# All blocks of the first modulation as split products, some rounding remainders and sums of squares on GpSimd, and a fifth key unit in the start stage

## The chip, the cores and the metric

One core of one Trainium2 chip. The time is the device time of one execution in microseconds. The kernel before took 2806.58 us in the median of 3 runs (2803.66 to 2813.95). TensorE is called PE in the profile, VectorE DVE, ScalarE ACT, GpSimd POOL, and SyncE SP. SP issues every DMA of the kernel.

## The reference, cut to what matters

Two transformer blocks on 256 tokens of 2048 features. The change touches only the beginning of the first one: the modulation vectors, the RMS norms of the tokens `x` and of the context `ctx`, and the key product.

```python
silu_c, silu_cc = silu(c), silu(c_ctx)[None]
mod_l = split(silu_c  @ w_mod + b_mod, 6)      # w_mod: 2048 x 12288
mod_c = split(silu_cc @ w_mod + b_mod, 6)
hl = rms_norm(x,   norm1_g) * (1 + mod_l[1]) + mod_l[0]
hc = rms_norm(ctx, norm1_g) * (1 + mod_c[1]) + mod_c[0]
zl  = hl @ w_in + b_in                         # w_in: 2048 x 13312
zkv = hc @ w_in[:, K_OFF:G_OFF] + b_in[K_OFF:G_OFF]
```

Only the first third of `w_mod` (`mod[0]` and `mod[1]`, 4096 columns) is needed before `hl` and `hc` exist. Nothing else of the two blocks can start before those.

## The kernel before

All weights come in blocks of 128x1024 f32 (512 KB), one DMA each, in an order that `unit_plan` writes out. A weight block for a token product is called a unit. It is multiplied as a split product: ACT rounds the block to fp32r (`his`, the first part, line 986), DVE subtracts that from the block (`los`, the second part, line 1570), and PE adds up `hi*xh + hi*xl + lo*xh` (lines 531, 533 and 536). PE takes the units in the order of the plan. There are 5 buffers each for `his` and `los`, so ACT waits before unit u until PE has finished unit u-5.

**The start stage.** The plan's first `NSTART` entries are the start stage. It holds the 64 blocks of the first third of `w_mod`, in 8 rounds of 8 blocks (one round for each `nb` of `MOD0 = (0, 4, 1, 5, 2, 6, 3, 7)`, q = 0 to 7 inside it), and the first halves of the first `NLEAD = 4` key units (`w_in` 40 to 43). The order before is 48 blocks (rounds 0 to 5), key unit 40, round 6, key unit 41, round 7, key units 42 and 43; then come the second halves of the same four units and everything else. I number plan entries b0, b1, and so on.

A round is computed in one of two ways, block by block (lines 612 to 646):

- q = 2 and q = 5 (`WHOLE`, 16 blocks, name `mod0`): PE takes the f32 block as it landed, with a 128x2 stationary operand, two f32 matmuls of 512 columns (line 627). Their end frees the block's buffer (`s_m0p`).
- the other six (48 blocks, name `mods`): split like a unit. PE multiplies `hi` and `lo` with the four columns of `CS` (the two silu vectors, each in two parts), four fp32r matmuls of 512 columns (line 639). The second part's end on DVE frees the buffer (`s_lo`).

After a round, ACT copies four rows out of PSUM (`mrow`, line 1048), PE turns them into columns (`mod0_turn`, line 603, eight small matmuls into the bank `XB`), and DVE adds `b_mod` (`modv`, lines 1668 and 1669).

**The norms.** ACT squares `x` and then `ctx`, four pieces of 128x1024 each (line 1034, `squares`). PE sums them over partitions with a matrix of ones: 16 f32 matmuls of 256 columns for `x` and 16 for `ctx` (line 589, into `XB`). ACT takes the root (line 1016), DVE the reciprocal (line 1650), and DVE multiplies the 16 feature rows (line 1656). Modulation (line 1700 on DVE, 1063 on ACT, 1681 on DVE) then makes four feature rows at a time, in four groups g = 0 to 3; group g needs rounds 2g and 2g+1 of `MOD0` order. The first half of a key unit needs groups 0 and 1, the second half groups 2 and 3.

**What sets the order.** Every engine runs a fixed program. Small tasks are generators that `Ticks.tick` moves on by one step after each plan entry, so a task's place in an engine's queue is the entry number at which its step falls. `early_times` says how many first parts (ACT, `AHEAD = 3` entries ahead) and second parts (DVE, 2 ahead) stand before the tick of an entry. The raw blocks go round 9 buffers in the start stage and 4 after it; SP issues the DMAs in plan order and waits before each for the buffer's last reader. The four `acc` banks, `S0`, `S1`, `TB` and `XB` are the eight PSUM banks. GpSimd has nothing to do in the start stage; its first work is the addition of attention masks much later (line 2338).

Of the kernel before, what the change touches and what calls it, by code (L numbers as in the profile page):

```python
# [25 lines left out]
WHOLE = (2, 5)  # L26
NEARLY, NLEAD = 48, 4
NSTART = 64 + NLEAD
FIRST = 64 - 8 * len(WHOLE) + NLEAD
# [75 lines left out]
def unit_plan():  # L105
# [14 lines left out]
    mod0 = [("mod0" if q in WHOLE else "mods", nb, q) for nb in MOD0 for q in range(8)]  # L120
# [54 lines left out]
def early_times(plan, lead):  # L175

    places = [i for i in range(NSTART) if plan[i][0] != "mod0"]
    at, n = [], 0
    for i in range(NSTART):
        seen = sum(p <= i for p in places)  # L180
        upto = min(len(places), seen + lead)
        at.append(places[n:upto])
        n = max(n, upto)
    return at
# [37 lines left out]
def build(nc, ar, out_d):  # L222
    ctx = ExitStack()
    with ctx:
# [104 lines left out]

        ident = cst[:, C_ID:C_ID + 128]  # L330
# [17 lines left out]
        def sumv(total, n):  # L348
# [9 lines left out]
        s_hi, s_lo, s_unit, s_mod, s_modt, s_modv = (  # L358
            sem(f"s_{n}") for n in ("hi", "lo", "unit", "mod", "modt", "modv"))
# [6 lines left out]
        s_m0p, s_m0e, s_m0t, s_m0v, s_mx, s_hx, s_lx, s_cs, s_sqx = (  # L366
            sem(f"s_{n}") for n in ("m0p", "m0e", "m0t", "m0v", "mx", "hx", "lx", "cs", "sqx"))
# [24 lines left out]
        act_early, dve_early = early_times(plan, AHEAD), early_times(plan, AHEAD - 1)  # L392
        unit_no, place_of, raw_free = {}, [], {}
        n_mod = n_m0p = 0
        raw_at, load_no, before, loads, last = [], [], [], [0] * (NRAW + NEXTRA), {}
        for i, key in enumerate(plan):
# [6 lines left out]
            if key[0] == "mod":  # L403
                n_mod += 1
                raw_free[i] = (s_mod, n_mod)
            elif key[0] == "mod0":
                n_m0p += 1
                raw_free[i] = (s_m0p, n_m0p)
            else:
                unit_no[key] = len(place_of)  # L410
                place_of.append(i)
                raw_free[i] = (s_lo, len(place_of))
# [24 lines left out]
        def _(e):  # L437
            nxt = 0

            def block_in():  # L440
# [4 lines left out]
                src = ar["w_mod"][m, h] if name in ("mod", "mod0", "mods") else ar[name][m, h]  # L445
# [58 lines left out]
        def _(e):  # L504
# [11 lines left out]
            def unit(b, k0, parts, start, stop, ready=None):  # L516
# [9 lines left out]
                for k in range(KU):  # L526
# [3 lines left out]
                    for i, (xh, xl, o) in enumerate(parts(k0 + k)):  # L530
# [3 lines left out]
                        if k + i == 0:  # L534
                            e.wait_ge(s_lo, j + 1)
# [76 lines left out]
            for i in range(NSTART):  # L612
                name, nb, q = plan[i]
                if name == "w_in":
                    b = opened(bank[nb - 40])
# [7 lines left out]
                if name == "mod0":  # L623
                    e.wait_ge(*landed(i))
                    for j in range(2):
                        k = 2 * q + j
                        mm = e.matmul(b.ap[0:2, :], vt[:, SC + 2 * k:SC + 2 * k + 2],
                                      raws[raw_at[i]][:, 512 * j:512 * j + 512], start=False, stop=False,
                                      skip_group_check=True)
                    mm.then_inc(s_m0p, 1)  # L630
                else:
                    unit_at += 1
                    u = unit_at
                    for part, ready in ((his, s_hi), (los, s_lo)):
                        w = part[u % NSPLIT][:, :, :].rearrange("p k m -> p (k m)")
                        e.wait_ge(ready, u + 1)
                        for j in range(2):
                            k = 2 * q + j
                            mm = e.matmul(b.ap[:, :], CS[:, 4 * k:4 * k + 128], w[:, 512 * j:512 * j + 512],
                                          start=(q == j == 0 and part is his), stop=(q == 7 and j == 1 and part is los),  # L640
# [1827 lines left out]
```

## Time and profile before

| what | value |
|---|---|
| median of 3 runs | 2806.58 us (2803.66 to 2813.95) |
| the profiled execution | 2808.74 us |
| its span, first to last instruction | 2806.9 us |
| PE busy | 2705.8 us, 96% |
| DVE busy | 1914.6 us, 68% |
| ACT busy | 1269.0 us, 45% |
| POOL busy | 188.1 us, 7% |
| mean granted PE clock | 0.981 |

The share of PE says that the kernel as a whole is bound by matmuls, but it is an average. The start stage, the first 5% of the span, is where PE is least busy and where all that the change touches lies. So the views that count are those of the first 160 us: the busy time of each engine by stretch, the groups of instructions by shape, the instructions in order of time on PE and on DVE, and the waits of SP's queue.

### The profile page before, as it was taken

The page shows a single profiled execution, that of the slowest core. Times are in us where ns is not written, and L with a number is a line of the kernel's source. Part 1 is how long each engine was busy: PE and PEld are TensorE (multiplying, and loading weights), DVE is VectorE, ACT ScalarE, POOL GpSimd, SP SyncE. Part 2 cuts the span into 40 slices and gives each one's busy share as a digit, 9 for nine tenths or more (in the row PEclk, how much of TensorE's full clock was granted, in tenths as well). Part 3 has the DMA queues.
Part 4 walks back from the last instruction along what each step waited for, and adds up shares of the span by engine and source line. Part 5 has one row for each costly group of instructions (what it writes and reads, how often), then busy time and mean ns, then how long its engine had stood idle before and what let it go on. Part 6 is the DMA issues. An engine that isn't in the chain of part 4 may idle for free.

```text
span 2806.9 us, 51478 instructions
## 1 busy us (share of the span) xinstructions
PE 2705.8 (96%) x21438; PEld 2581.1 (92%) x21438; DVE 1914.6 (68%) x2951; ACT 1269.0 (45%) x1827; POOL 188.1 (7%) x180
## 2 busy tenths in 40 slices
PE   7999999899999999999999999999999998979996
PEld 4599977798999999999999999999999998979996
DVE  6765667789998777875555645677566656487564
ACT  5522344553444545544443434464444444444453
POOL 0000011000014000100000000030000000220011
PEclk9999999999999999999999999999999999989998
DMA  8766633456876777776555555554344443535563
GB/s 310 270 229 222 204 115 112 143 188 205 273 239 223 248 265 263 258 255 205 183 191 183 181 192 183 188 187 152 135 155 146 151 150 128 175 104 180 181 200 108
DMA packets 163991, 539.02 MB, mean 192 GB/s; under 512 B 31024, under 2 KB 35120, under 8 KB 163632
## 3 DMA queue, kind: packets, MB, share of 16 engines
q1 hardware_dynamic: 163760, 535.73, 57.3%
q8 instruction: 170, 2.79, 0.4%
q14 instruction: 61, 0.50, 0.0%
HBM read 533.57 MB, written 2.10 MB: 191 GB/s over the span
## 4 chain that ended last, share of the span: by engine, by line
PE 62%; DVE 5%; issue 1%; ACT 1%; POOL 0%; POOLq 0%; ACTq 0%; DVEq 0%
PE ps L531 20%; PE ps L536 19%; PE ps L533 19%; DVE lo L1570 1%; DVE row L2137 1%; PE ps L865 0%; DVE AL L2213 0%; PE ps L887 0%; PE ps L888 0%; PE ps L569 0%; DVE H L2221 0%; DVE ON L2145 0%; DVE Z L2301 0%; PE ps L960 0%; PE ps L959 0%
## 5 line engine op out<-in xcount | busy, mean ns | idle before, releaser
L986 ACT ACTIVATE hi<-raw 128x1024 fp32r<-128x1024 f32 x856 | 902.0, 1059 | 954.3 <-PE ps L536 463.2
L531 PE MATMUL ps<-AH,hi 128*128 128x256 f32 (+2 forms) x4480 | 1283.5, 287 | 13.7 <-DVE AL L2213 13.7
L536 PE MATMUL ps<-AH,lo 128*128 128x256 f32 (+2 forms) x4480 | 1270.4, 284 | 9.5 <-DVE lo L1570 9.5
L533 PE MATMUL ps<-AL,hi 128*128 128x256 f32 (+2 forms) x4480 | 1269.4, 283 | 0.0
L1570 DVE TENSOR_TENSOR lo<-raw,hi 128x1024 fp32r<-128x1024 f32 x856 | 1036.0, 1224 | 201.3 <-ACT hi L986 198.9
L531 PEld LDWEIGHTS ps<-AH,hi 128*128 128x128 f32 x4480 | 850.4, 190 | 45.8 <-issue 34.6
L536 PEld LDWEIGHTS ps<-AH,lo 128*128 128x128 f32 x4480 | 849.9, 190 | 12.3 <-DVE lo L1570 12.3
L533 PEld LDWEIGHTS ps<-AL,hi 128*128 128x128 f32 x4480 | 851.2, 190 | 1.0
L531 PE MATMUL ps<-YH,hi 128*128 128x256 f32 (+1 forms) x1536 | 433.8, 282 | 6.5 <-DVE YL L2148 6.5
L536 PE MATMUL ps<-YH,lo 128*128 128x256 f32 (+1 forms) x1536 | 432.9, 282 | 0.0
L533 PE MATMUL ps<-YL,hi 128*128 128x256 f32 (+1 forms) x1536 | 432.5, 282 | 0.0
L531 PEld LDWEIGHTS ps<-YH,hi 128*128 128x128 f32 x1536 | 290.8, 189 | 7.7 <-DVE YL L2148 7.6
L536 PEld LDWEIGHTS ps<-YH,lo 128*128 128x128 f32 x1536 | 291.6, 190 | 0.0
L533 PEld LDWEIGHTS ps<-YL,hi 128*128 128x128 f32 x1536 | 290.0, 189 | 0.0
L2320 POOL TENSOR_TENSOR ssum<-ssum,sqr 128x256 f32<-128x256 f32 (+1 forms) x112 | 117.1, 1045 | 256.1 <-ACT sqr L1007 252.2
L1851 DVE SCALAR_TENSOR_TENSOR CV<-U,vec,CV 128x256 f32<-128x256 f32 x240 | 118.1, 492 | 4.3
L2317 POOL COPY ssum<-sqr 128x272 f32<-128x272 f32 (+1 forms) x16 | 9.1, 575 | 1487.6 <-ACT sqr L1007 1487.6
L536 PE MATMUL ps<-BH,lo 128*128 128x256 f32 x384 | 107.5, 280 | 1.0 <-DVE lo L1570 1.0
L531 PE MATMUL ps<-BH,hi 128*128 128x256 f32 x384 | 107.5, 280 | 0.0
L533 PE MATMUL ps<-BL,hi 128*128 128x256 f32 x384 | 107.0, 279 | 0.0
L1997 DVE TENSOR_TENSOR tmp<-ps,rown 128x256 f32<-128x256 f32 x64 | 27.2, 424 | 114.2 <-PE ps L536 114.2
L2019 DVE SCALAR_TENSOR_TENSOR H<-ps,modv,H 128x256 f32<-128x256 f32 x48 | 23.3, 485 | 116.5 <-PE ps L536 116.5
(253 smaller groups left out, 2493.2 us busy)
## 6 DMA issues: line engine op xcount, KB each, us to landing
raw<-in_w_ff SPq DMA_DIRECT2D x256, 512.0 KB, 4.1
raw<-in_w_in SPq DMA_DIRECT2D x208, 512.0 KB, 4.4
raw<-in_w_mod SPq DMA_DIRECT2D x192, 512.0 KB, 4.7
raw<-in_w_ain SPq DMA_DIRECT2D x128, 512.0 KB, 3.6
raw<-in_w_pin SPq DMA_DIRECT2D x64, 512.0 KB, 3.5
raw<-in_w_o SPq DMA_DIRECT2D x32, 512.0 KB, 4.7
raw<-in_w_aout SPq DMA_DIRECT2D x32, 512.0 KB, 3.5
raw<-in_w_pout SPq DMA_DIRECT2D x32, 512.0 KB, 4.3
```

What stands on the lines that cost most here:

```text
L531: e.matmul(b.ap[:, o], hi[:, k, :], xh, start=start and k + i == 0, stop=False, skip_group_check=many)
L533: e.matmul(b.ap[:, o], hi[:, k, :], xl, start=False, stop=False, skip_group_check=many)
L536: mm = e.matmul(b.ap[:, o], los[j % NSPLIT][:, k, :], xh, start=False, stop=stop and k == KU - 1, skip_group_check=many)
L986: e.activation(his[u % NSPLIT][:, :, :], raws[raw_at[i]][:, :].rearrange("p (k m) -> p k m", k=KU), ACT.Copy).then_inc(s_hi, 1)
L1570: e.tensor_tensor(los[u % NSPLIT][:, :, :], raws[raw_at[i]][:, :].rearrange("p (k m) -> p k m", k=KU), his[u % NSPLIT][:, :, :].bitcast(F3 ...
L1851: o = e.scalar_tensor_tensor(out=CV[:, m, :], in0=U[:, m, w:w + T], scalar=s, in1=CV[:, m, :], op0=ALU.mult, op1=ALU.add)
L1997: e.tensor_tensor(x[:, 0:T], b[:, 0:T], rown[:, 0:T], ALU.mult).then_inc(*own.up())
L2019: e.scalar_tensor_tensor(out=H[:, m, NM:L], in0=(tmp[m % 3] if c == 3 else b)[:, 0:T], scalar=g, in1=H[:, m, NM:L], op0=ALU.mult, op1=ALU. ...
L2137: e.reciprocal(r[:, 0:L], r[:, 0:L]).then_inc(*own.up())
L2317: e.tensor_copy(dst, src).then_inc(s_add, 1)
L2320: e.tensor_tensor(dst, dst, src, ALU.add).then_inc(s_add, 1)
```

## The change

- All 64 blocks of the first modulation are split; the two-column f32 product and its semaphore are gone.
- Of the blocks with q = 2 and q = 5, the ten from the fourth round on (`modg`) get their second part from GpSimd instead of DVE, with a semaphore of its own, `s_log`. PE and SP wait for `s_log` there. DVE passes over them.
- GpSimd first adds the pieces of squares in pairs (four additions of 128x1024), so PE sums 8 matmuls for `x` and 8 for `ctx` in place of 16 each. PE's sum for `x` comes after 10 plan entries (before: 7) and that for `ctx` 7 entries later (before: 4); the roots and reciprocals are moved to match.
- `NEARLY, NLEAD` goes from 48, 4 to 40, 5. The first key unit comes after five rounds, one more after each of the sixth and seventh, and two after the eighth; the fifth (`w_in` 44) uses the bank `TB`.
- `lead` in `early_times` is now counted in plan entries, all of which are split.

```diff
-WHOLE = (2, 5)
-NEARLY, NLEAD = 48, 4
+POOLED, NDVE = (2, 5), 24
+NEARLY, NLEAD = 40, 5
 NSTART = 64 + NLEAD
-FIRST = 64 - 8 * len(WHOLE) + NLEAD
+FIRST = NSTART
...
-    mod0 = [("mod0" if q in WHOLE else "mods", nb, q) for nb in MOD0 for q in range(8)]
+    mod0 = [("modg" if q in POOLED and 8 * n + q >= NDVE else "mods", nb, q)
+            for n, nb in enumerate(MOD0) for q in range(8)]
...
+        acc_kv = acc + [TB] + [acc[i % 4] for i in range(11)]
...
-                    for _ in range(6 - 3 * c):
+                    for _ in range(9 - 3 * c):
                         yield
                     opened(xb)
-                    for k in range(16):
+                    for k in range(8):
                         if k % 4 == 0:
-                            e.wait_ge(s_sqx, 4 * c + k // 4 + 1)
-                        mm = e.matmul(XB[:, 0:T], ones[2048][:, :], squares[4 * c + k // 4][:, k % 4, :],
-                                      start=(k == 0), stop=(k == 15))
+                            e.wait_ge(s_sqa, 2 * c + k // 4 + 1)
+                        mm = e.matmul(XB[:, 0:T], ones[2048][:, :], squares[4 * c + k // 4 * 2][:, k % 4, :],
+                                      start=(k == 0), stop=(k == 7))
...
-                if name == "mod0":
-                    e.wait_ge(*landed(i))
                     for j in range(2):
                         k = 2 * q + j
-                        mm = e.matmul(b.ap[0:2, :], vt[:, SC + 2 * k:SC + 2 * k + 2],
-                                      raws[raw_at[i]][:, 512 * j:512 * j + 512], start=False, stop=False,
-                                      skip_group_check=True)
-                    mm.then_inc(s_m0p, 1)
...
+                yield
+                yield
+                root(rows[ROW["x"] % 2], T)
+                for _ in range(7):
+                    yield
+                root(rows[ROW["ctx"] % 2], T)
+                for _ in range(4):
+                    yield
...
-                    for _ in range(8 if key == "x" else 1):
+                    for _ in range(10 if key == "x" else 2):
                         yield
...
                 for p in dve_early[i]:
-                    second_part(p)
+                    if plan[p][0] != "modg":
+                        second_part(p)
...
+            for i in (0, 2, 4, 6):
+                e.wait_ge(s_sqx, i + 2)
+                e.tensor_tensor(squares[i], squares[i], squares[i + 1], ALU.add).then_inc(s_sqa, 1)
+            for i in range(NSTART):
+                if plan[i][0] == "modg":
+                    u = number_at[i]
+                    e.wait_ge(s_hi, u + 1)
+                    e.tensor_tensor(los[u % NSPLIT][:, :, :], raws[raw_at[i]][:, :].rearrange("p (k m) -> p k m", k=KU),
+                                    his[u % NSPLIT][:, :, :].bitcast(F32), ALU.subtract).then_inc(s_log, 1)
```

## Rows read from the trace of the kernel before

**Rows 1.** Busy time by stretch: us from:to, length, PE, PEld, DVE, ACT, POOL, clock, DMA share, GB/s.

```profile
0.00:153.90 153.90, 133.76 (x578) 84.60 (x579) 100.15 (x188) 80.14 (x106) 0.20 (x4) 0.94 0.76 283
153.90:400.00 246.10, 246.10 (x1984) 228.24 (x1983) 153.14 (x217) 76.96 (x107) 11.21 (x9) 1.00 0.60 198
...
70.00:75.00 5.00, 4.57 (x12) 2.49 (x13) 5.00 (x10) 3.46 (x5) 0.00 (x0) 0.53 0.84 338
```

**Rows 2.** Waits of SP's queue in the first 160 us: total us, times, longest.

```profile
SPq L448 <- PE ps L627: 77.7, 15, 12.1
SPq L448 <- DVE lo L1570: 37.6, 15, 8.1
```

**Rows 3.** PE in order of time: start us, us, what, count, idle before and its releaser.

```profile
38.92 1.27 PE L603 MATMUL ps<-comb,mrow 4*128 4x2 f32 x8 [4.14 <-ACT mrow L1048]
...
43.32 7.17 PE L589 MATMUL ps<-upon,ones 128*128 128x256 f32 x32
...
58.99 1.88 PE L627 MATMUL ps<-raw,vt 128*2 128x512 f32 x4
60.80 0.74 PE L639 MATMUL ps<-hi,CS 128*128 128x512 f32 x2
...
70.43 1.22 PE L639 MATMUL ps<-lo,CS 128*128 128x512 f32 x2 [1.25 <-DVE lo L1570]
71.58 1.86 PE L603 MATMUL ps<-comb,mrow 4*128 4x2 f32 x8
73.38 3.58 PE L627 MATMUL ps<-raw,vt 128*2 128x512 f32 x4
76.88 0.82 PE L639 MATMUL ps<-hi,CS 128*128 128x512 f32 x2
...
81.87 0.63 PE L639 MATMUL ps<-hi,CS 128*128 128x512 f32 x2
...
83.72 0.63 PE L639 MATMUL ps<-hi,CS 128*128 128x512 f32 x2
...
141.90 0.28 PE L531 MATMUL ps<-AH,hi 128*128 128x256 f32 x1
...
147.43 1.05 PE L603 MATMUL ps<-comb,mrow 4*128 4x2 f32 x8
```

**Rows 4.** DVE in order of time, same columns.

```profile
38.34 1.75 DVE L1650 RECIPROCAL row<-row 128x256 f32<-128x256 f32 x1 [2.46 <-ACT row L1016]
40.01 1.16 DVE L1570 TENSOR_TENSOR lo<-raw,hi 128x1024 fp32r<-128x1024 f32 x1
...
45.03 1.43 DVE L1656 TENSOR_TENSOR VTok<-H,row 128x256 f32<-128x256 f32 x4
46.37 1.22 DVE L1570 TENSOR_TENSOR lo<-raw,hi 128x1024 fp32r<-128x1024 f32 x1
47.51 1.43 DVE L1656 TENSOR_TENSOR VTok<-H,row 128x256 f32<-128x256 f32 x4
...
65.71 0.41 DVE L1700 TENSOR_SCALAR tmp<-G,vt,modv 128x256 f32<-128x256 f32 x1
66.04 0.42 DVE L1681 TENSOR_TENSOR AL<-tmp,AH 128x256 fp32r<-128x256 f32 x1
66.38 0.41 DVE L1681 TENSOR_TENSOR CL<-tmp,CH 128x256 fp32r<-128x256 f32 x1
```

**Rows 5.** GpSimd's two-input additions with no DVE work beside them: us, names, shape.

```profile
324.00 1.01 POOL L2338 TENSOR_TENSOR Bt<-Bt,cst 128x384 f32<-128x384 f32 x1 [0.70 <-DMA Bt<-in_rpb]
...
478.91 0.73 POOL L2320 TENSOR_TENSOR ssum<-ssum,SGV 128x256 f32<-128x256 f32 x1 [1.88 <-DVE SGV L1787]
```

**Rows 6.** DVE and GpSimd at the same time, in order of time.

```profile
799.74 1.22 DVE L1570 TENSOR_TENSOR lo<-raw,hi 128x1024 fp32r<-128x1024 f32 x1
799.90 1.67 POOL L2360 TENSOR_TENSOR G<-G,tmp 128x256 f32<-128x256 f32 x1 [283.40 <-DVE tmp L1920]
800.88 1.24 DVE L1589 SCALAR_TENSOR_TENSOR macc<-raw,vt,macc 128x512 f32<-128x512 f32 x1
802.15 0.75 DVE L1592 SCALAR_TENSOR_TENSOR macc<-raw,vt,macc 128x512 f32<-128x512 f32 x1
```

More of the change, by code:

```diff
@@ L172, in unit_plan, with early_times @@
     return plan
-def early_times(plan, lead):
-    places = [i for i in range(NSTART) if plan[i][0] != "mod0"]
+def early_times(lead):
     at, n = [], 0
     for i in range(NSTART):
[L180 to L183, printed above, removed]
+        upto = min(NSTART, i + 1 + lead)
+        at.append(range(n, upto))
+        n = upto
     return at
@@ L411, in build @@
                 place_of.append(i)
-                raw_free[i] = (s_lo, len(place_of))
+                if key[0] == "modg":
+                    n_pooled += 1
+                    low_made.append((s_log, n_pooled))
+                else:
+                    n_low += 1
+                    low_made.append((s_lo, n_low))
+                raw_free[i] = low_made[-1]
         number_at = {i: j for j, i in enumerate(place_of)}
@@ L622, in _ @@
                     opened(b)
-                if name == "mod0":
-                    e.wait_ge(*landed(i))
+                unit_at += 1
+                u = unit_at
+                for part, ready in ((his, (s_hi, u + 1)), (los, low_made[u])):
+                    w = part[u % NSPLIT][:, :, :].rearrange("p k m -> p (k m)")
+                    e.wait_ge(*ready)
                     for j in range(2):
                         k = 2 * q + j
-                        mm = e.matmul(b.ap[0:2, :], vt[:, SC + 2 * k:SC + 2 * k + 2],
-                                      raws[raw_at[i]][:, 512 * j:512 * j + 512], start=False, stop=False,
+                        mm = e.matmul(b.ap[:, :], CS[:, 4 * k:4 * k + 128], w[:, 512 * j:512 * j + 512],
+                                      start=(q == j == 0 and part is his), stop=(q == 7 and j == 1 and part is los),
                                       skip_group_check=True)
-                    mm.then_inc(s_m0p, 1)
[L631 to L640, printed above, removed]
-                                          skip_group_check=True)
-                    mm.then_inc(s_unit, 1)
+                mm.then_inc(s_unit, 1)
                 if q == 7:
@@ L672, in _ @@
                 if m < NLEAD:
-                    unit(bank[m], KU, both, False, True, (lambda k: e.wait_ge(s_lx, 2 * k + 2)) if m == 0 else None)
-                    bank[m].free = (s_k, m + 1)
-                    tile_at = m + 1
+                    b = (bank + [tb])[m]
+                    unit(b, KU, both, False, True, (lambda k: e.wait_ge(s_lx, 2 * k + 2)) if m == 0 else None)
+                    b.free = (s_k, m + 1)
+                    tile_at = 0
                 else:
@@ L680, in _ @@
             finish(*ticks.active)
+            tile_at = 0
             def attend(u):
@@ L1035, in norms @@
                         yield
-                for key in ("x", "ctx"):
-                    root(rows[ROW[key] % 2], T)
-                    for _ in range(4):
-                        yield
+                yield
[6 more added lines that the diff above has]
+                    yield
                 have.add("ctx")
```

29 lines of the change are left out of this document (13 added, 16 removed).

## The prediction

> **What bounds the kernel now.** I read busy time by stretch first. After 153.9 us PE is busy without a gap for the next 246 us [rows 1]; there the time is a sum of matmuls, and nothing in the change alters them except that one half unit moves forward. Before 153.9 us PE is busy for 133.8 of 153.9 us, partly at a reduced clock (mean granted 0.94), and DVE for 100.2 us [rows 1]. So the change is worth what it does to one moment: the end of the start stage, when PE begins the second half of key unit 40. That moment is 153.9 us: the last turn of a round starts at 147.43 and takes about 1.0, and one key unit is 141.90 to 147.43 less that turn's lead-in, 5.45 us (48 matmuls at a pitch of 0.1135) [rows 3].
>
> Next I asked what each engine waits for inside it. SP waits 77.7 us for PE's two-column products and 37.6 us for DVE [rows 2]: buffers of the f32 blocks come free only in PE's turn, and loads come late. In order of time PE shows one large hole and two kinds of stretch. The hole lies before 50 us: 4.14 us idle for ScalarE's root, then a turn, one f32 block and 7.17 us of ones-matmuls for ctx [rows 3]. From there DVE sets the pace (reciprocals, rows of the norm and second parts back to back, rows 4) until about 71 us, and after it PE itself does, at a low clock after each pair of gaps: the granted clock is 0.53 from 70 to 75 us [rows 1], and a turn takes 1.86 us and an f32 block 3.58 us there, against about 1.0 and 1.88 [rows 3].
>
> **PE's load.** An f32 block occupies PE for 60.80-58.99 = 1.81 us. Two split blocks take 83.72-81.87 = 1.85, so 0.93 each [rows 3]. Sixteen blocks change, which takes off 16 x 0.88 = 14.1 us. The ones-matmuls halve: 7.17 us for one tensor [rows 3], twice, gives 7.2 us back. Together PE has 21.3 us less to do. That is the ceiling of the gain and would be 0.76%. A fifth key unit adds 5.45 us to the stage and takes it off the rest, nothing in sum.
>
> **DVE's and GpSimd's load.** A second part takes 47.51-46.37 = 1.14 us of DVE [rows 4]. Sixteen more are made, six of them on DVE (6.8 us) and ten on GpSimd. For GpSimd's price I have additions of 256 and 384 elements without DVE beside them, 0.73 and 1.01 us [rows 5]: a slope of 0.28/128 = 2.2 ns an element. For 1024 this gives an estimate of 0.73 + 768 x 0.0022 = 2.4 us. The upper bound is the contended 1.67 us for 256 elements [rows 6] times four, 6.7 us; the lower bound is a price equal to DVE's 1.14. I take 2.4, since the rows without DVE beside them give the work itself and the contended one also holds a wait for DVE.
>
> How the two share comes from rows 6. GpSimd's 0.73 us addition, dispatched 0.16 us into a DVE second part, lasts 1.67 us; the DVE product after it lasts 1.24 us where its twin lasts 0.75. So GpSimd began when DVE's instruction ended, and DVE's next began when GpSimd's ended: they took turns. This is the rule of the Trainium skill (SBUF — State Buffer, "Who interferes with whom"): a DVE instruction with two SBUF inputs and a GpSimd instruction that reads SBUF block each other for a whole instruction. By that rule a second part moved to GpSimd costs a busy DVE 2.4 us instead of 1.14, and speaks against the move; were there no exclusion, the move would save DVE 1.14 each time.
>
> DVE's one-input modulation products (0.325 us each, 66.04-65.71, rows 4) I take to run beside GpSimd; no row shows it.
>
> **Edits at no cost.** The four additions of squares (4 x 2.4 us) fall before about 38 us, while DVE waits for loads (2.46 us idle before its first reciprocal at 38.34, rows 4); they push second parts back by 1 to 3 us, and the sum for x is moved back by three entries anyway. Sixteen more first parts on ScalarE (about 1 us each) lie in its waits: it is busy 80.1 of 153.9 us [rows 1], which leaves 74 us. SP's wait turns from PE to DVE and GpSimd, which finish a block earlier than PE does; behind a late GpSimd block all later loads queue, but nine buffers give over 10 us. The rotation of banks and TB wait for nobody: 5 second halves (27 us) lie between.
>
> **The sum, in steps.**
>
> A. PE does ten blocks, then half a ones-sum (3.6 us), and ScalarE's root follows 14 first parts instead of the earlier place. I estimate the root's end at 40.5 (before, 38.3).
>
> B. From there DVE has work without a gap up to the second part of b40, the first key unit. Two reciprocals at 40.01-38.34 = 1.67 make 3.3. Thirty-two norm rows at (46.37-45.03)/4 = 0.335 make 10.7. Of b13 to b40, 24 blocks at 1.14 make 27.4. Sixteen modulation products (for k = 0 to 7) at 0.325 make 5.2, and twelve remainders at 0.335 (0.67 for a pair, rows 4) make 4.0. Small ones make 0.8. Four GpSimd blocks at 2.4, less about 2 that falls beside one-input work, make 7.4. One short wait for a turn is 0.5. Sum 59.3, so 99.8. PE has little to do meanwhile and waits.
>
> C. PE ends key unit 40 at 99.8 + 5.3 = 105.1.
>
> D. The sixth round is PE's: 8 x 0.93 + 1.0 for a turn = 8.45, then key unit 41 (5.45), then one block and a turn (1.93): 120.9. GpSimd's two blocks lie in DVE's waits for that turn.
>
> E. Now group 2 is modulated, and DVE leads again until b58, key unit 42: five second parts 5.7, eight products 2.6, six remainders 2.0, small ones 0.5, one GpSimd block less its cover 1.5: 12.3, so 133.2.
>
> F. PE: 5.3, then 8.45 (seven blocks of round 7 and one more, with a turn), unit 43 5.45, the last turn 1.0, unit 44 5.45: 158.9.
>
> Less the half unit that moved, 5.45, this stands at 153.4 against 153.9: a gain of 0.5 us. The exclusive time is somewhat less than the sum of durations (neighbours in time order overlap by about 0.1 us, as 799.74 + 1.22 and 800.88 do, rows 6), 0.1 for each of 6 on the path: 0.6 more. So 1.1 us less than before. The profiled execution took 2808.74, 2.2 over the median shown, and its span 2806.9; the change makes it 2807.6, and on the median's basis 2805.5.
>
> The reason so little comes of 21.3 us of relieved PE is that steps B and E, 71.6 of 159 us, are DVE's, and DVE is given six second parts and up to 2.4 us for each GpSimd block that falls among them.
>
> **Rivals.**
>
> 1. GpSimd's work runs beside DVE's, or finds its pauses. For: the hole of ScalarE's waits, and GpSimd chooses its moment. Against: rows 6. Step B loses 7.4 us; the turn of round 3 then comes earlier, which adds nothing more. PE, though, waits for b26 and b29 for about 2 us, and step E loses 1.5 us. That gives 7 us in all: 2799.
>
> 2. The low clock. PE now waits through step B in many small gaps, and the clock fell after gaps in rows 3 (0.53 in rows 1) for about 6.5 us, where work took twice its time, a loss of 3.3 us. Before it hit PE's own rounds, as at 70 us; now it would hit key units 40 and 42 right after steps B and E. Twice 3.3 us against the sum: 2812. For: the same pattern of gaps. Against: those losses are in the 153.9 already, and PE at half clock still keeps pace with DVE in step B (1.86 against 2.5 us a block).
>
> 3. Slower than before: GpSimd is the bound. If a second part of 1024 elements takes 6.7 us there (the contended row times four), PE stands at each of the five blocks in B and E (b26, b29, b34, b37, b55) and DVE is shut out that long: 5 x 4.3 = 21 us more, 2826. It decides from 2.4 + 1.1/5 = 2.6 us on: beyond that the change loses. Over 5.4 us it loses more than 14.
>
> 4. PE is relieved for good: the waits of SP for PE (77.7 us) were the true limit, the loads come early, DVE starts its row of work 5 us sooner and there is no exclusion. Then 15 to 18 us of the 21.3 arrive: 2790. Against: between 40 and 48 us and at 65 to 67 us DVE runs one operation behind the other [rows 4], so its sum in B isn't made of waits for loads. That the change doesn't act at all isn't likely: 16 blocks must take one of the two paths.
>
> **How the numbers follow.** The forecast 0.46, rival 1 0.20, rival 2 0.16, rival 3 0.07 (half of it, prices between 2.6 and 5.4 us, still within 0.5%), rival 4 0.11. 0.5%, which is 14 us, is about what a measurement of this kernel can tell from no change. Faster by more than that is rival 4: 0.11. Slower is the far half of rival 3 and rival 2 on top of a dear GpSimd: 0.06. The rest, 0.83, is within it. The range leaves out rival 4 and the far part of 3, and takes in rivals 1 and 2 with some 3 us of error in step A and the median's own spread: 2795 to 2815.
>
> **What would show each step.** The profile after should have: ones-matmuls of 3.6 us for a tensor and 256 split records in place of 192 and 64; GpSimd's 128x1024 operations near 2.4 us when alone and up to 3.6 when dispatched into a DVE second part, and DVE second parts of 2 us and more behind them; the root for x at 40, b40's second part at 100; DVE busy over 19 of 20 us between 40 and 100; SP waiting for DVE and GpSimd only; the second half of key unit 40 starting at 159. The prediction is wrong if b40's second part comes before 94 (rival 1 or 4), if PE's clock is low inside a key unit (rival 2), or if PE waits over 2 us for a GpSimd block (rival 3).

## The result, and the profile after

| | before | after |
|---|---|---|
| median | 2808.72 us | 2827.61 us |
| runs from and to | 2801.99 to 2813.95 us | 2823.24 to 2831.54 us |
| after over before | | 1.0069 [1.0055, 1.0083] |
| profiled execution, its span | 2808.74, 2806.9 us | 2830.1, 2828.3 us |
| mean granted clock | 0.981 | 0.977 |
| start of the last turn of a round | 147.43 us | 166.63 us, less the half unit 161.2 |
| span less that last turn | 2659.5 us | 2667.1 us, counted alike |

The change costs 19 us. The forecast was 1.1 us less than before, with a range up to 2815, so the result is slower and outside it. In the two profiled executions the stage ends 161.18 - 147.43 = 13.8 us later, and the rest takes 7.6 us longer, though the forecast said that nothing in the change alters it. Each kernel has one profiled execution. The unchanged kernel profiled again had its last turn at 144.32, so a difference of two last turns is good to about 3 us.

Busy time by stretch in the profile after; the columns are those of [rows 1]. The first stretch is the start stage, the last one runs from DVE's first reciprocal to the end of b40's second part:

```profile
0.00:173.10 173.10, 132.51 (x592) 102.79 (x593) 126.14 (x195) 96.21 (x123) 50.46 (x18) 0.86 0.73 255
80.00:85.00 5.00, 4.90 (x15) 4.27 (x16) 5.00 (x13) 4.50 (x6) 2.04 (x1) 0.50 0.68 216
85.00:90.00 5.00, 2.18 (x8) 1.41 (x6) 4.31 (x4) 2.22 (x3) 5.00 (x1) 0.84 0.22 84
90.00:95.00 5.00, 3.43 (x8) 2.76 (x9) 0.00 (x0) 1.46 (x2) 2.49 (x2) 0.50 0.47 157
...
43.45:109.87 66.42, 47.57 (x158) 33.36 (x156) 56.08 (x98) 36.80 (x51) 16.21 (x5) 0.79 0.65 221
```

PE is busy for 132.5 of 173.1 us; it was 133.8 of 153.9 [rows 1]. The stage has a half unit of 5.45 us more, so PE was relieved of 6.7 us of busy time and not of 21.3. The clock explains the difference in size: its mean over the stage is 0.86 where it was 0.94, which I estimate at 0.14 x 173.1 - 0.06 x 153.9 = 15 us at full clock, PE's idle time included. And where PE was relieved, it then waited. Read 80 to 95 us as one event: DVE full while GpSimd holds an instruction, then GpSimd busy while all of DVE stands, and the clock at half speed around it.

SP's waits in the first 165 us have turned from PE [rows 2] to DVE and GpSimd, as forecast, and are no shorter in sum (122 us against 117); behind one GpSimd block the loads queued for 10 us:

```profile
SPq L452 <- DVE lo L1571: 93.6, 46, 5.3
SPq L452 <- POOL lo L2343: 28.6, 7, 10.0
```

GpSimd in order of time (start us, us, what, idle before and its releaser). Of its ten second parts (line 2343) six last 2.39 to 2.52 us, one 3.34 and three over 6:

```profile
21.17 2.47 POOL L2338 TENSOR_TENSOR under<-under 128x1024 f32<-128x1024 f32 x1 [20.73 <-ACT under L1031]
24.95 3.14 POOL L2338 TENSOR_TENSOR under<-under 128x1024 f32<-128x1024 f32 x1 [1.31 <-ACT under L1031]
...
76.04 2.52 POOL L2343 TENSOR_TENSOR lo<-raw,hi 128x1024 fp32r<-128x1024 f32 x1 [37.95 <-ACT hi L983]
82.96 8.55 POOL L2343 TENSOR_TENSOR lo<-raw,hi 128x1024 fp32r<-128x1024 f32 x1 [4.40 <-ACT hi L983]
94.02 2.39 POOL L2343 TENSOR_TENSOR lo<-raw,hi 128x1024 fp32r<-128x1024 f32 x1 [2.51 <-ACT hi L983]
...
109.55 6.19 POOL L2343 TENSOR_TENSOR lo<-raw,hi 128x1024 fp32r<-128x1024 f32 x1 [8.35 <-ACT hi L983]
...
144.29 6.36 POOL L2343 TENSOR_TENSOR lo<-raw,hi 128x1024 fp32r<-128x1024 f32 x1 [6.02 <-ACT hi L983]
```

DVE in order of time, same columns:

```profile
42.17 0.16 DVE L1669 TENSOR_TENSOR modv<-ps,vec 128x4 f32<-128x4 f32 x1 [2.99 <-PE ps L607]
...
43.45 1.74 DVE L1651 RECIPROCAL row<-row 128x256 f32<-128x256 f32 x1
...
60.77 1.75 DVE L1651 RECIPROCAL row<-row 128x256 f32<-128x256 f32 x1 [2.33 <-ACT row L1013]
...
75.94 0.40 DVE L1701 TENSOR_SCALAR tmp<-G,vt,modv 128x256 f32<-128x256 f32 x1
76.27 2.45 DVE L1701 TENSOR_SCALAR tmp<-VTok,vt,modv 128x256 f32<-128x256 f32 x1
...
82.22 1.21 DVE L1571 TENSOR_TENSOR lo<-raw,hi 128x1024 fp32r<-128x1024 f32 x1
83.35 0.41 DVE L1682 TENSOR_TENSOR AL<-tmp,AH 128x256 fp32r<-128x256 f32 x1
...
84.36 0.41 DVE L1682 TENSOR_TENSOR CL<-tmp,CH 128x256 fp32r<-128x256 f32 x1
84.70 4.62 DVE L1571 TENSOR_TENSOR lo<-raw,hi 128x1024 fp32r<-128x1024 f32 x4
95.69 1.81 DVE L1571 TENSOR_TENSOR lo<-raw,hi 128x1024 fp32r<-128x1024 f32 x1 [6.38 <-ACT hi L983]
99.06 0.16 DVE L1669 TENSOR_TENSOR modv<-ps,vec 128x4 f32<-128x4 f32 x1 [1.56 <-PE ps L607]
...
99.21 3.07 DVE L1571 TENSOR_TENSOR lo<-raw,hi 128x1024 fp32r<-128x1024 f32 x1
...
108.66 1.21 DVE L1571 TENSOR_TENSOR lo<-raw,hi 128x1024 fp32r<-128x1024 f32 x1
...
112.28 1.21 DVE L1571 TENSOR_TENSOR lo<-raw,hi 128x1024 fp32r<-128x1024 f32 x1
...
146.05 2.34 DVE L1571 TENSOR_TENSOR lo<-raw,hi 128x1024 fp32r<-128x1024 f32 x2
```

PE in order of time:

```profile
54.77 5.46 PE L593 MATMUL ps<-upon,ones 128*128 128x256 f32 x16
...
80.10 1.84 PE L607 MATMUL ps<-comb,mrow 4*128 4x2 f32 x8 [3.61 <-ACT mrow L1049]
...
91.57 1.22 PE L634 MATMUL ps<-lo,CS 128*128 128x512 f32 x2 [4.39 <-POOL lo L2343]
...
109.93 0.58 PE L540 MATMUL ps<-AH,lo 128*128 128x256 f32 x1 [1.49 <-DVE lo L1571]
...
116.83 1.05 PE L607 MATMUL ps<-comb,mrow 4*128 4x2 f32 x8
...
131.52 1.05 PE L607 MATMUL ps<-comb,mrow 4*128 4x2 f32 x8
...
151.75 1.05 PE L607 MATMUL ps<-comb,mrow 4*128 4x2 f32 x8
...
166.63 1.05 PE L607 MATMUL ps<-comb,mrow 4*128 4x2 f32 x8
```

**The event at 83 us.** GpSimd is given b29 (line 2343) at 82.96, while DVE is inside a second part. DVE goes on, one second part or remainder behind the other, until 89.3, and GpSimd's operation ends at 91.5, 2.2 us later. The other two long ones end alike: 109.55 + 6.19 = 115.74 is 2.25 us behind the end of DVE's row (112.28 + 1.21), and 144.29 + 6.36 = 150.65 is 2.26 behind (146.05 + 2.34). That is about the length of the operation alone, so I read that each did its work only after DVE's row had ended. At 83 us PE waits 4.39 us for it, ScalarE for PE, and DVE stands for 6.38 us. So a 2.4 us subtraction held the kernel's three other computing engines in turn. They did take turns, but not one for one as in [rows 6].

### The profile page after: what moved, and what is told of

It is laid out like the page before. It is cut to its first block, busy times and chain, and to the rows that moved or that the text cites. A ratio compares the mean times of both kernels' runs of the same rounds, so it can differ in the third digit from the quotient of the medians.

```text
span 2828.3 us, 51467 instructions
## 1 busy us (share of the span) xinstructions
PE 2705.4 (96%) x21406; PEld 2600.3 (92%) x21406; DVE 1940.5 (69%) x2957; ACT 1281.4 (45%) x1843; POOL 237.3 (8%) x194
## 4 chain that ended last, share of the span: by engine, by line
PE 61%; DVE 5%; issue 1%; ACT 1%; POOL 0%; POOLq 0%; ACTq 0%; DVEq 0%
PE ps L535 19%; PE ps L540 19%; PE ps L537 19%; DVE lo L1571 1%; DVE row L2139 1%; PE ps L862 0%; DVE AL L2215 0%; PE ps L884 0%; PE ps L885 0%; DVE H L2223 0%; PE ps L573 0%; DVE ON L2147 0%; DVE Z L2303 0%; PE ps L956 0%; PE ps L957 0%
## 5 line engine op out<-in xcount | busy, mean ns | idle before, releaser
L983 ACT ACTIVATE hi<-raw 128x1024 fp32r<-128x1024 f32 x872 | 916.1, 1057 | 948.5 <-PE ps L540 470.6
L1571 DVE TENSOR_TENSOR lo<-raw,hi 128x1024 fp32r<-128x1024 f32 x862 | 1057.4, 1241 | 205.5 <-ACT hi L983 203.3
L540 PEld LDWEIGHTS ps<-AH,lo 128*128 128x128 f32 x4480 | 850.6, 190 | 15.8 <-DVE lo L1571 15.8
```

What stands on the lines that cost most here:

```text
L540: mm = e.matmul(b.ap[:, o], los[j % NSPLIT][:, k, :], xh, start=False, stop=stop and k == KU - 1, skip_group_check=many)
L983: e.activation(his[u % NSPLIT][:, :, :], raws[raw_at[i]][:, :].rearrange("p (k m) -> p k m", k=KU), ACT.Copy).then_inc(s_hi, 1)
L1571: e.tensor_tensor(los[u % NSPLIT][:, :, :], raws[raw_at[i]][:, :].rearrange("p (k m) -> p k m", k=KU), his[u % NSPLIT][:, :, :].bitcast(F3 ...
```

## The experiments

The questions were two: what the stage lost, and what the rest lost.

**All second parts on DVE** (the rival that the number of split blocks, not GpSimd, is at fault, against GpSimd's ten).

```diff
-POOLED, NDVE = (2, 5), 24
+POOLED, NDVE = (), 24
```

> The changed kernel with all ten second parts back on DVE; GpSimd only adds the pairs of squares. Theory A (GpSimd's second parts are what costs: it and DVE shut each other out, and PE waits for the late block): the last turn of a round, at 166.6 us in the changed kernel, comes 9 to 12 us earlier, at 155 to 158, and the median is 2816 to 2820 against 2827.6. Rival B (DVE is simply overloaded by split blocks, GpSimd is a relief): ten more second parts of 1.14 us on DVE make it later, 2827 to 2835. Rival C (the low clock after PE's gaps is the loss, whoever makes the second parts): within 2 us of 2827.6.

Measured: median 2821.11, ratio 1.0044 [1.0029, 1.0059]. The last turn starts at 155.68, 11 us earlier than with GpSimd, and every product of line 1701 is short again, by the groups of that line (ns min/median/max, first and last start in us):

```profile
155.68 1.05 PE L607 MATMUL ps<-comb,mrow 4*128 4x2 f32 x8
```

```profile
L1701 DVE TENSOR_SCALAR tmp<-VTok,vt,modv x16: 406/408/417, 72.6 to 162.1; 128x256 f32<-128x256 f32 x16
L1701 DVE TENSOR_SCALAR tmp<-G,vt,modv x16: 404/409/414, 72.9 to 162.4; 128x256 f32<-128x256 f32 x16
```

So in these executions GpSimd's ten blocks are 11.0 of the stage's 13.8 us. By the medians, 2827.61 against 2821.11, they are 6.5 us: the profiled execution here took 2816.17, the fastest of its four, so 11 is the upper end. Less the half unit, this kernel's last turn is at 150.2, 2.8 us behind before and 5.9 behind before's second profile: with all blocks split on DVE the stage isn't faster either.

**Ghost operations**: all second parts on DVE, and besides, ten GpSimd operations of the same number of elements, each released by the same first part, that read constants and write a scratch tile (in bf16) for which nobody waits until the stage is over. All of the computation is there; the ten are work on top.

```diff
+            n_ghost, ghost = 0, cst[:, 0:512].unsqueeze(1).broadcast_to([128, 2, 512])
...
-                if plan[i][0] == "modg":
+                if plan[i][0] == "mods" and plan[i][2] in (2, 5) and 8 * MOD0.index(plan[i][1]) + plan[i][2] >= 24:
...
                     e.wait_ge(s_hi, u + 1)
...
+                    e.tensor_tensor(GB[:, :, :], ghost, ghost, ALU.subtract).then_inc(s_ghost, 1)
```

> As all_dve, but GpSimd also runs ten additions of 128x1024 for which nobody waits, each released by the same first part that released its second part in the changed kernel; they read constants and write a scratch tile. It parts the two halves of theory A. If the loss is DVE being shut out while GpSimd holds the way to SBUF (2.4 us each where DVE is busy), the time is near the changed kernel's or above it, 2824 to 2832, since DVE now has ten more second parts too. If the loss is PE waiting for a late GpSimd block, it is as fast as all_dve, within 2 us. In either case PE waits for no GpSimd work in the start stage.

Measured: median 2827.05, ratio 1.0073 [1.0052, 1.0094]; last turn at 164.48, 8.8 us behind the kernel without ghosts. GpSimd and, in a fence of its own, DVE in order of time:

```profile
82.07 16.38 POOL L2351 TENSOR_TENSOR GB<-cst 128x1024 bf16<-128x1024 f32 x3 [4.40 <-ACT hi L985]
...
106.41 6.83 POOL L2351 TENSOR_TENSOR GB<-cst 128x1024 bf16<-128x1024 f32 x1 [7.96 <-ACT hi L985]
...
122.00 1.99 POOL L2351 TENSOR_TENSOR GB<-cst 128x1024 bf16<-128x1024 f32 x1 [4.25 <-ACT hi L985]
```

```profile
75.83 1.98 DVE L1704 TENSOR_SCALAR tmp<-VTok,vt,modv 128x256 f32<-128x256 f32 x1
77.74 0.40 DVE L1704 TENSOR_SCALAR tmp<-G,vt,modv 128x256 f32<-128x256 f32 x1
```

DVE's second parts up to the end of the stage, with ghosts and without (busy us, mean ns):

```profile
L1574 DVE TENSOR_TENSOR lo<-raw,hi 128x1024 fp32r<-128x1024 f32 x70 | 96.4, 1409 | 7.3 <-ACT hi L985 7.3
L1571 DVE TENSOR_TENSOR lo<-raw,hi 128x1024 fp32r<-128x1024 f32 x70 | 89.8, 1317 | 7.4 <-ACT hi L983 7.4
```

Nobody waits for a ghost, so these 8.8 us (5.9 by the medians) are DVE shut out. The same seventy second parts last 6.6 us longer in sum, and the one-input products and the small instructions of line 1694 another 6.4: one product takes 1.98 us in place of 0.41. GpSimd's lateness, for which PE waits in the kernel after, is then the smaller part: 2 of 11 us by the turns and 0.6 of 6.5 by the medians, both less than these differences are good to. A ghost is also a little shorter than a real second part (1.99 alone against 2.4), so its effect is rather too small than too large. The new tile moves no other, as it is created last in a stack of tiles that is closed at once; the rest, 2665.5 us, is that of the kernel without ghosts (2664.2). A GpSimd operation that takes 1.99 alone lasts 6.83 beside DVE's row.

**Fewer of them, where PE leads**: GpSimd takes blocks in the sixth and eighth rounds only, four in all.

```diff
-"modg" if q in POOLED and 8 * n + q >= NDVE else "mods"
+"modg" if q in POOLED and n in (5, 7) else "mods"
```

> The changed kernel with GpSimd's second parts in the sixth and eighth round alone (four of them), where DVE has nothing to modulate and waits for PE's turn; the other six are on DVE. Theory A: equal to all_dve or up to 3 us faster, since there is no collision on the path. Rival B: between the changed kernel and all_dve in the other direction (slower than the changed kernel). Rival C: 2827 within 2 us.

Measured: 2820.9, ratio 1.0047 [1.0032, 1.0062], last turn 158.69, 3.0 us behind no GpSimd at all, which is no more than the scatter. Its four operations last 6.18, 2.45, 6.37 and 2.45 us: the first of each round still meets a row of DVE's. Nothing separates this median from that without GpSimd, so even there the move gained nothing; the forecast's claim in step D, that GpSimd's blocks there lie in DVE's waits, holds for every second one.

**A break in DVE's row**: the kernel after, with a memset of one column on DVE behind each of its second parts from b24 on. The first form put it into a new tile of 288 bytes a partition.

```diff
         sb("pad", [128, 16])
+        BUB = sb("BUB", [128, 72])
...
+                if 24 <= i < NSTART:
+                    e.memset(BUB[:, i:i + 1], 0.0)
```

> The changed kernel with one tiny DVE memset (128x1, no SBUF input) after each of DVE's second parts from b24 on. Theory A1 (a waiting GpSimd addition gets in only when DVE's next instruction is not another one with two SBUF inputs; hence additions of 8.55, 6.19 and 6.36 us): the longest addition falls to 3.7 us or less, PE's wait of 4.4 us for one is gone, and the time falls by 3 to 6 us, to 2822 to 2825. Theory A2 (it has to wait for a stretch in which DVE is really idle): the long additions stay and the time is the same or 1 us more.

Measured: 2843.45, ratio 1.0126 [1.0111, 1.0141], but the last turn at 159.43, 7.2 us earlier than in the kernel after, and no GpSimd second part over 3.43 us. So the stage gained as expected, and the whole was 18 us above the expected range: the rest lost 19 us more, 2686.6 from the last turn (less the half unit) to the end. The new tile had moved the addresses of others, which led to the next experiment, and to the same one with no new tile, the memsets going into unused columns of tiles that are there:

```diff
-        sb("pad", [128, 16])
+        PADT = sb("pad", [128, 16])
...
+                if 24 <= i < NSTART:
+                    c = n_bub.pop(0)
+                    e.memset(PADT[:, c:c + 1] if c < 16 else vt[:, 216 + c:217 + c], 0.0)
```

> The run with a tiny DVE memset behind each second part once more, now with the memsets going to unused columns of tiles that exist, so that no tile moves (in the first such run, the new tile alone would account for the 16 us by which it was slower, as an unused tile of the same size cost 18 us in the kernel before). Theory A1 (a waiting GpSimd addition gets in when DVE's next instruction is no second-part-like one) with the address effect gone: GpSimd's additions 3.5 us or less, last turn at 159 to 161 instead of 166.6, time 2819 to 2823. Rival: the first run's earlier last turn was an effect of the addresses too: last turn at 165 to 168, time 2826 to 2830.

Measured: 2821.97, ratio to before 1.0054 [1.0037, 1.0071] against the 1.0069 of the change, 5.6 us less by the medians; last turn 162.41, 4.2 us earlier. GpSimd in order of time, then DVE:

```profile
82.20 2.71 POOL L2347 TENSOR_TENSOR lo<-raw,hi 128x1024 fp32r<-128x1024 f32 x1 [4.41 <-ACT hi L983]
...
139.99 3.42 POOL L2347 TENSOR_TENSOR lo<-raw,hi 128x1024 fp32r<-128x1024 f32 x1 [6.02 <-ACT hi L983]
```

```profile
81.45 1.21 DVE L1571 TENSOR_TENSOR lo<-raw,hi 128x1024 fp32r<-128x1024 f32 x1
82.60 2.59 DVE L1686 TENSOR_TENSOR AL<-tmp,AH 128x256 fp32r<-128x256 f32 x1
82.61 0.06 DVE L1575 MEMSET pad<- 128x1 f32 x1
```

The same block as at 82.96 above takes 2.71 us in place of 8.55: GpSimd gets in at the memset, and the remainder behind it waits. A GpSimd second part of 2.4 us lasts 6 to 8 because DVE's two-input instructions follow one another without a break; with a memset between, none lasts more than 3.42. That gives back some 4 of the 11 us; that the others stay because GpSimd's own 2.4 us still shut DVE out is what the ghosts show.

**An unused tile in the kernel before** (does an address alone cost time?). No instruction changes. First the 288 bytes behind `pad`, then `pad` itself 64 bytes longer.

```diff
         sb("pad", [128, 16])
+        sb("BUB", [128, 72])
```

> The kernel before with an unused tile of 288 bytes per partition allocated behind the pad tile, so that the weight buffers and most other tiles lie 288 bytes higher; no instruction is changed. In the run with the memsets all stretches after the start stage ran at 86 to 88 matmuls in 10 us where the kernel before reaches 90 to 91 in many. Theory D (the pace of PE's matmul stream depends on where the tiles lie): the pace is 86 to 88 nearly everywhere and the time rises by 10 to 25 us, to 2817 to 2832. Rival (the pace is set by timing, whatever the addresses): 2806.6 within 4 us.

Measured: 2826.31, ratio 1.0065 [1.005, 1.008].

```diff
-        sb("pad", [128, 16])
+        sb("pad", [128, 32])
```

> The kernel before with the pad tile 64 bytes longer (128 instead of 64), nothing else. Theory D1 (any shift of the tiles behind it takes the fast pace away, the old length being one that happens to suit): 2820 to 2830, at most 88 matmuls in 10 us. Theory D2 (it depends on the amount; 288 bytes is bad, small amounts aren't): 2808 within 3 us.

Measured: 2836.46, ratio 1.0104 [1.0088, 1.012]. The first lies in the range expected of moved tiles, the second above it. The stage ends as in before's second profile (last turns 144.95 and 143.64), and the rest is late by 22 and 27 us. Busy time by stretch, one stretch from each of before, the first form, the second form and, for comparison, the kernel after:

```profile
280.00:310.00 30.00, 30.00 (x265) 30.00 (x264) 20.37 (x27) 6.38 (x8) 0.00 (x0) 1.00 0.63 215
```

```profile
280.00:310.00 30.00, 30.00 (x257) 30.00 (x256) 19.61 (x26) 5.89 (x7) 0.00 (x0) 1.00 0.59 201
```

```profile
280.00:310.00 30.00, 30.00 (x256) 30.00 (x255) 19.75 (x26) 5.39 (x6) 0.00 (x0) 1.00 0.59 196
```

```profile
280.00:310.00 30.00, 30.00 (x265) 30.00 (x264) 17.84 (x24) 6.46 (x7) 0.00 (x0) 1.00 0.60 209
```

PE is full and its granted clock is 1.00 in all four, and yet it does 265, 257, 256 and again 265 matmuls in 30 us. So where tiles lie can cost as much as a change. It is not what the change itself costs: its diff creates no tile, so none is moved, and the kernel after keeps before's count here.

**Is the rest's loss the same effect?** The kernel before once more, unchanged:

> The kernel before, unchanged, profiled once more to see how far the last turn (147.4) and the rest after it (2659.5 us) move from execution to execution. If the 5 to 8 us that the changed kernel loses after the start stage are such scatter, this profile shows a last turn within 1 us and a rest that differs by 5 us or more; if the rest stays within 2 us, they belong to the changed kernels.

Measured: 2806.88, last turn 144.32, rest 2660.7 against 2659.5. The turn, expected within 1 us, differs by 3 between two executions, and the rest by about 1. Then the buffers `his` and `los` renamed in a ring, which changes which buffer, and so which address, each block of the rest has, in before (by two) and in after (by three):

```diff
+        his, los = (t[2:] + t[:2] for t in (his, los))
```

> The kernel before with the five his and los buffers renamed in a circle by two (unit u uses buffer (u+2) mod 5), and nothing else. The change makes 17 more units before the rest of the kernel begins, so that every later unit moves on by 17 mod 5 = 2 buffers. Theory G (which of the five buffers a unit has, against the four raw buffers, the activations and the banks, sets the pace of PE's matmuls; that is where the changed kernel loses the 5 to 8 us after the start stage): the last turn stays at 147.4 within 1 us, and the time is 2813 to 2819. Rival H (the rest of the kernel is slower for another reason, such as its later start or the bank of the fifth key unit): 2808 within 2 us.

> The changed kernel with the same buffers renamed by three, so that every unit after the start stage has the very buffer it had in the kernel before. Theory G: last turn at 166.6 within 1 us as in the changed kernel, and the rest of the kernel 5 to 8 us shorter: 2819 to 2823. Rival H: 2827.6 within 2 us.

Measured: before renamed 2806.67, ratio 0.9995 [0.9986, 1.0005], last turn 143.67, rest 2657.5; after renamed 2828.2, ratio 1.0073 [1.0058, 1.0088], last turn 167.27, rest 2665.1. The theory of the buffers fell: neither median moves as it forecast. Three profiles of before's instructions have a rest of 2657.5 to 2660.7 and two of after's one of 2665.1 and 2667.1, so 4 to 10 us aren't scatter.

The traces tell where they are lost. Counted from the last turn less the half unit, the last product of the tile `CH` starts at 166.3 to 166.4 us in the three profiles of before and at 167.2 and 166.4 in the two of after: so far the rest is as before. The first product of the tile `YH` starts at 927.3 to 928.2 in before, at 934.1 and 931.9 in after, and at 931.4 with all second parts on DVE. From there to the end it is 1733 us in both of after and 1730.2 to 1733.3 in before. So the rest's loss falls more than 166 us behind the stage, and it falls without GpSimd's second parts as well.

**The fifth key unit alone**: all second parts on DVE, and four units as before.

```diff
-NEARLY, NLEAD = 40, 5
+NEARLY, NLEAD = 48, 4
...
-        acc_kv = acc + [TB] + [acc[i % 4] for i in range(11)]
+        acc_kv = acc * 4
```

> The kernel all_dve with the old order of key units: 48 blocks, then four key units instead of five (and the old banks). It isolates the fifth key unit and its place. Theory A expects nothing from it in the start stage: the last turn at 150 to 153 (155.7 in all_dve less the 5.45 us of one half unit), time 2816 to 2822 as all_dve's 2821. Rival E (the earlier key unit hides DVE's lag, by giving PE work while DVE catches up): the last turn comes at 153 or later and the time is 3 to 6 us above all_dve's. Rival F (the fifth unit delays the modulation behind it): 3 to 6 us below.

Measured: 2817.9, ratio 1.0037 [1.0024, 1.0051]; last turn 151.28 against 155.68 - 5.45 = 150.2 with five, rest 2663.3 against 2664.2. The fifth unit changes nothing in the stage beyond the execution's scatter, and is not what slows the rest.

**The additions of squares alone**, in the kernel before, with the moved sums, roots and reciprocals (cut to the additions):

```diff
...
+            for i in (0, 2, 4, 6):
+                e.wait_ge(s_sqx, i + 2)
+                e.tensor_tensor(squares[i], squares[i], squares[i + 1], ALU.add).then_inc(s_sqa, 1)
```

> The kernel before (f32 blocks on PE as they were, four key units) with only GpSimd's four additions of squares, half the ones-matmuls, and the sums, roots and reciprocals at the places of the changed kernel. My step A said that these additions are free. Then PE has 7.2 us less in the hole before 50 us, of which 2 to 6 us reach the last turn (147.4 before, now 141 to 145), and the time is 2800 to 2805. Rival: DVE leads from 40 us on, begins its reciprocal 2 us later, and the last turn is at 147 to 149, the time 2807 to 2811.

Measured: 2809.32, ratio 1.0007 [0.9997, 1.0016]. In all they cost and bring nothing that the interval (-0.03% to 0.16%) can tell, though PE has 7 us less to do. In the stage they don't look free: the last turn is at 149.96, 2.5 and 5.6 us behind the two profiles of before, where 141 to 145 was expected. DVE's row of work begins late, since the sums were moved back (in before its first reciprocal starts at 38.34):

```profile
44.59 1.74 DVE L1655 RECIPROCAL row<-row 128x256 f32<-128x256 f32 x1
```

That delay is in every kernel with the moved sums: their first reciprocal starts at 41.5 to 44.6, those of the kernels without at 37.9 to 38.6. So part of what the stage loses with all second parts on DVE may be this one and not the split blocks.

**A mixed version**: the kernel before with the pairs; blocks stay f32 in the rounds where DVE leads and are split, on DVE, in the first, sixth and eighth, where PE does. No GpSimd second parts, four units.

```diff
+ROUNDS = (1, 2, 3, 4, 6)
...
-    mod0 = [("mod0" if q in WHOLE else "mods", nb, q) for nb in MOD0 for q in range(8)]
+    mod0 = [("mod0" if q in WHOLE and n in ROUNDS else "mods", nb, q) for n, nb in enumerate(MOD0) for q in range(8)]
```

> The kernel before with the pairs of squares and with the f32 blocks split only in the first, sixth and eighth round, where DVE has slack and PE leads; in the five rounds where DVE leads q = 2 and q = 5 stay f32 blocks on PE. GpSimd makes no second parts. If my account of the stages is right, PE loses 4 x 0.88 = 3.5 us in rounds six and eight and up to 5 us by the pairs, nothing is put on DVE where it leads: last turn at 139 to 144, time 2798 to 2804. If any split block in the place of an f32 block costs, it is above 2807.

> The kernel mixed, which has 6 more units than the kernel before, with the buffers renamed by four, so that the later units have the buffers of the kernel before. Its last turn was at 141.3, 6.2 us ahead of the kernel before. Theory G: the rest takes as long as in the kernel before and the gain arrives: 2799 to 2802. Rival H: 2806.9 within 2 us, as mixed.

Measured: 2806.85 against 2808.24 beside it, ratio 0.9989 [0.998, 0.9999]; with the buffers renamed by four, 2805.68, ratio 1.0001 [0.9992, 1.001]. The last turn starts at 141.26 and 140.54: 3 to 7 us are gained in the stage over the executions of before (144.32 to 147.43), as forecast (139 to 144). The rest is 2664.2 and 2661.3, and takes most of it back, so that the time missed its forecast of 2798 to 2804. This is the only arrangement with more split blocks that isn't slower than before, and it is at best 0.1% faster. Two neighbours price the splitting: the pairs alone have the last turn at 149.96, 9 us later, and the kernel with every block split on DVE and four units has it at 151.28, 10 us later. Splitting gained in the three rounds where PE leads and lost in the five where DVE does.

## Why the prediction was wrong, point by point

**What bounds the kernel.** Right that the start stage decides the sign, and wrong in that "nothing in the change alters" the rest. The rest, counted from the last turn, was late by 7.6 us in the kernel after, and by 4 to 5 in those that split more blocks on DVE alone (all on DVE 2664.2, four units 2663.3, mixed 2664.2, though mixed renamed has 2661.3). The renamed buffers, the fifth unit and scatter don't account for it, and moved tiles can't, as the change moves none. The cause stays open.

**Step A**, the root for x at 40.5: it ended at 41.03. Right to half a microsecond, and the squares cost GpSimd 2.46 to 3.14 us each. That "DVE has work" from there was not right: its row began at 43.45, and the experiment with the pairs alone shows the same late start (44.59) with no split block added. "No cost" holds for the time in all, not for the stage.

**Step B**, b40's second part at 99.8: it ended at 109.87, 10.1 us late. This step failed. The window of 43.45 to 109.87 splits it. DVE was busy 56.1 us in it, where the sum of 59.3, less its half microsecond of waiting, has 58.8: 2.7 us less, so the work itself was priced enough. The 2.7 are GpSimd's: the DVE instructions that it lengthened, at 76.27, 95.69 and 99.21, hold about 4.5 us beyond their usual length, where the step had 7.4 for four blocks; b29, the second of the four, worked while DVE stood. What was missing is idle time. The row began at 43.45, not 40.5, since DVE's instruction for the first turn (line 1669) and a second part stand ahead of the reciprocal, and the former waits 2.99 us for PE: 2.9 us. And inside it DVE stood 2.33 + 6.38 + 1.56 = 10.3 us, where the step had 0.5. The 2.33 come from the ones-sum for ctx: 5.46 us for 16 matmuls where I halved a row to 3.6; with the pairs alone, at a granted clock of 1.00, the same 16 take 3.62, and here PE was partly at the low clock. The 6.38 follow from b29's late addition; the 1.56, the wait for the next turn of a round, I only argue to be its echo. In sum 2.9 + 9.8 - 2.7 = 10.0, so the failed term is the step's "one short wait" of 0.5 us, which measured 10.3.

Of three claims under it two were wrong, each by a row:
- "They took turns" [rows 6] was read as one for one. There the addition came between two instructions and cost one turn. Against an unbroken row of DVE's it is passed over until the row ends: 8.55, 6.19 and 6.36 us (8.55, 6.20 and 6.36 in the renamed kernel), and 2.71, 2.57 and 3.42 for the same three with memsets in the row.
- "I take to run beside GpSimd; no row shows it", of the one-input products. One lasts 2.45 us at 76.27, as long as GpSimd's operation beside it; the ScalarE work behind it is late, and PE waits 3.61 us at 80.10, where with all second parts on DVE it waits 2.23. The G product behind each long one took 0.40. The Trainium skill (SBUF — State Buffer, "Who interferes with whom") says that an instruction with one SBUF input doesn't contend except in the faster two-port modes, which `tensor_scalar` can enter. The 2.45 and the ghost's 1.98 us fit the exception. The Trainium skill says in the same section that whoever issues first gets the shared ports for the whole instruction, and read as one turn for each instruction, that has GpSimd wait for one. The trace differs at 82.96: GpSimd's waiting second part was served only after eight more DVE instructions.
- "GpSimd's price" was right: 2.39 to 2.52 us where it is alone, against 2.4 forecast from a slope over two smaller sizes [rows 5].

**Step C**, unit 40: 5.3 us forecast; from 109.93 to the turn at 116.83 it is 6.9, of which about 1.5 are the low clock's (mean granted 0.78 from 109.93 to 117.00), which step C left out and rival 2 had named.

**Step D**, 15.8 us forecast for the sixth round and unit 41: the turns start at 116.83 and 131.52, so with the turn's own 1.05 it is 15.7. Right, though GpSimd's first block there lasts 6.19 us: PE has key matmuls to do meanwhile.

**Steps E and F**: 38.0 us forecast, 173.1 - 132.6 = 40.5 measured. Up to the turn at 151.75 it is 19.2 against 17.6; in that part GpSimd's addition of 144.29 lasts 6.36 us and one of 134.93 lasts 3.34. From there it is 21.35 against 20.4, a size that I can't put to a cause.

**The rivals.** Rival 3, GpSimd as the bound, has the result's sign and nearly its size (2826 against 2827.6), but its mechanism is not what happened. It decided "from 2.6 us on", and GpSimd took 2.4 of work. What lasted 6 to 8 us was its wait, and the larger part of the loss is DVE's (8.8 us with ghosts that nobody waits for). It priced five stands of PE at 4.3 us each; PE stood so long for GpSimd once, 4.39 us at 91.57. Rival 2 is there in size (1.5 us at unit 40, 1.9 us at the ones-sum), but it is not what GpSimd's blocks cost: without them the mean granted clock of the stage is as low (0.87). Rivals 1 and 4 fell: the exclusion is real, and PE's relief brought no time. Rival 3's 0.07 was too low: the upper bound of 6.7 us came from a contended row, and I weighed it as a price of the operation, which [rows 5] made unlikely, not as a length of its wait, on which no row spoke against it.

## What to carry to other kernels

Moving a two-input elementwise operation to GpSimd can pay only where DVE has pauses (none of the arrangements run here gained by it), because it costs a busy DVE up to GpSimd's whole time, and a GpSimd instruction that meets an unbroken row of DVE's waits for the row's end, with everything that depends on it. Cost such a move by the longest unbroken row around each of its instructions, not by its own duration. Give an engine's relief a price only at the places where that engine leads: in the stage, splitting blocks paid only in the rounds where PE led. Profile the unchanged kernel twice before reading a few microseconds out of two traces: its own last turn moved by 3.

## What the runs showed that I had not expected

Addresses alone can cost more than the change. With no instruction altered, 64 bytes more in the unused tile `pad` made the kernel 1.04% slower, 288 bytes 0.65%, at a granted clock of 1.00 and with PE full (256 and 257 matmuls in 30 us where before has 265). Why, these runs don't tell. An experiment that adds a tile is therefore not a clean one: the first form with memsets gained 7 us in the stage and was 16 us slower in all; the second form, with no new tile, was 6 us faster in all.
